# A four-layer trunk on one core: the root's wait placed later, weight blocks split two ahead, high and low parts stored apart, scores of two heads in turn

## The reference

```python
for i in range(4):
    x = x + 0.5 * swiglu(rms_norm(x, g1[i]), w_gate1[i], w_up1[i], w_down1[i])   # D_FF = 2816
    h = rms_norm(x, g_mix[i])
    x = x + (fox, conv, diff, fox)[i](h)
    x = x + 0.5 * swiglu(rms_norm(x, g2[i]), w_gate2[i], w_up2[i], w_down2[i])

def swiglu(h, wg, wu, wd):
    return (silu(h @ wg) * (h @ wu)) @ wd

# fox, for each of 16 heads of 64 features, causal:
s = q @ k.T / 8 + cum[q] - cum[k];  o = softmax(s) @ v
# diff, for each of 8 heads with two score maps each:
a = softmax(s1) - lam * softmax(s2);  o = a @ v
```

## Time and profile before

| What | Value |
|---|---|
| time, median of 3 runs | 2146.58 us |
| time of the profiled execution | 2145.89 us |
| span in the profile | 2144.1 us |
| TensorE busy | 2059.0 us (96%) |
| VectorE busy | 1478.0 us (69%) |
| ScalarE busy | 1062.4 us (50%) |
| GpSimd busy | 118.6 us (6%) |
| DMA traffic | 344.28 MB, mean 161 GB/s |
| mean granted clock of TensorE | 0.982 |

### The profile page before, as it was taken

The page is one execution under the profiler, slowest core; times in us unless marked ns, Lnnn a source line. Parts: engine busy times, 40 slices in busy tenths (PEclk is TensorE's granted clock), DMA queues, the critical chain, the costliest instruction groups (busy, mean ns, idle before and its releaser), DMA issues.

```text
span 2144.1 us, 28806 instructions
## 1 busy us (share of the span) xinstructions
PE 2059.0 (96%) x12322; PEld 1792.1 (84%) x12322; DVE 1478.0 (69%) x1750; ACT 1062.4 (50%) x1243; POOL 118.6 (6%) x118
## 2 busy tenths in 40 slices
PE   6999999999999997799999999989999999999999
PEld 5888888888788896788878888878887888888887
DVE  6766766776677499577657747877756765767773
ACT  5554555554554430555445535665535554455552
POOL 1000201000100112100000000010000000101000
PEclk8999999999999998999999999999999999999999
DMA  6555434555555540355556563346555555334553
GB/s 200 183 185 168 138 119 138 161 189 182 174 182 185 189 155 0 104 171 184 175 172 196 172 201 122 114 138 189 180 186 172 180 179 185 126 99 144 190 181 114
DMA packets 329692, 344.28 MB, mean 161 GB/s; under 512 B 8277, under 2 KB 325214, under 8 KB 329566
## 3 DMA queue, kind: packets, MB, share of 16 engines
q1 hardware_dynamic: 329422, 342.41, 50.3%
q10 hardware_dynamic: 144, 0.05, 0.0%
HBM read 341.38 MB, written 1.05 MB: 160 GB/s over the span
## 4 chain that ended last, share of the span: by engine, by line
PE 90%; DVE 6%; ACT 2%; issue 2%; DMA 0%; DVEq 0%; SPq 0%
PE banks L1326 47%; PE banks L1321 23%; PE banks L1310 5%; PE banks L1312 4%; PE banks L1311 4%; DVE sb_w_low L727 2%; PE banks L1504 2%; DVE sb_x_square L1201 2%; PE banks L1552 1%; ACT sb_w_high L436 1%; PE banks L1519 1%; PE banks L1536 1%; PE banks L1507 1%; DMA sb_raw<-in_ffn_w_up 0%; PE banks L1650 0%
## 5 line engine op out<-in xcount | busy, mean ns | idle before, releaser
L1326 PE MATMUL banks<-sb_x_both,sb_w_high 128*128 128x512 f32 x2816 | 979.8, 401 | 45.9 <-DVE sb_w_low L727 38.8
L727 DVE TENSOR_TENSOR sb_w_low<-sb_raw,sb_w_high 128x2048 fp32r<-128x2048 f32 (+1 forms) x332 | 747.1, 2252 | 154.9 <-ACT sb_w_high L436 153.3
L1321 PE MATMUL banks<-sb_x_both,sb_w_low 128*128 128x256 f32 x2816 | 735.6, 282 | 0.0
L436 ACT ACTIVATE sb_w_high<-sb_raw 128x2048 fp32r<-128x2048 f32 (+1 forms) x332 | 617.1, 1863 | 125.8 <-DMA sb_raw<-in_ffn_w_down 106.6
L1326 PEld LDWEIGHTS banks<-sb_x_both,sb_w_high 128*128 128x128 f32 x2816 | 512.6, 191 | 146.7 <-issue 49.2
L1321 PEld LDWEIGHTS banks<-sb_x_both,sb_w_low 128*128 128x128 f32 x2816 | 540.1, 192 | 31.7
L1326 PE MATMUL banks<-sb_h_both,sb_w_high 128*128 128x512 f32 x1408 | 495.3, 398 | 1.9 <-DVE sb_w_low L727 1.9
L1321 PE MATMUL banks<-sb_h_both,sb_w_low 128*128 128x256 f32 x1408 | 386.1, 282 | 0.0
L1326 PEld LDWEIGHTS banks<-sb_h_both,sb_w_high 128*128 128x128 f32 x1408 | 261.7, 189 | 61.1 <-DVE sb_w_low L727 2.2
L1321 PEld LDWEIGHTS banks<-sb_h_both,sb_w_low 128*128 128x128 f32 x1408 | 265.1, 188 | 6.0
L1310 PE MATMUL banks<-sb_x_both,sb_w_high 128*128 128x256 f32 x512 | 149.5, 292 | 0.0
(11 more groups left out here) (205 smaller groups left out, 2083.4 us busy)
## 6 DMA issues: line engine op xcount, KB each, us to landing
sb_raw<-in_ffn_w_gate SPq DMA_DIRECT2D x88, 1024.0 KB, 5.3
sb_raw<-in_ffn_w_up SPq DMA_DIRECT2D x88, 1024.0 KB, 5.3
sb_raw<-in_ffn_w_down SPq DMA_DIRECT2D x64, 1024.0 KB, 5.2
sb_raw<-in_ffn_w_down SPq DMA_DIRECT2D x32, 768.0 KB, 4.8
sb_raw<-in_fox_w_in SPq DMA_DIRECT2D x24, 1024.0 KB, 5.3
sb_raw<-in_conv_w_pw SPq DMA_DIRECT2D x12, 1024.0 KB, 5.6
sb_raw<-in_diff_w_in SPq DMA_DIRECT2D x12, 1024.0 KB, 5.1
sb_raw<-in_fox_w_out SPq DMA_DIRECT2D x8, 1024.0 KB, 4.9
```

The costliest lines, as they stand in the source:

```text
L436: act.activation(slot(w_high, b)[:, 0:width(b)], slot(raw, b)[:, 0:width(b)], ACT.Copy).then_inc(S["high_ready"], 1)
L727: dve.tensor_tensor(slot(w_low, b)[:, 0:width(b)], slot(raw, b)[:, 0:width(b)], slot(w_high, b)[:, 0:width(b)].bitcast(F32), ALU.subtract) ...
L1321: pe.matmul(bank[at][:, SEQ:2 * SEQ], low[:, n * P:(n + 1) * P], m_both[:, 0, :], start=False, stop=False, skip_group_check=True)
L1326: ins = pe.matmul(pair(bank[at][:, :]), high[:, n * P:(n + 1) * P], m_both[:, :, :], start=first, stop=last, skip_group_check=True)
```

## The change

**The root's wait.** TensorE no longer waits for `root_ready` after the first pair, but before the last of the four tiles of the second pair (its up tile into bank 3).

**Two blocks ahead.** ScalarE splits b+2 and b+3 before the root, VectorE before the reciprocal. In the pair loop the splits are now b+2p+4 and b+2p+5, each behind the evacuation of one half (ScalarE) or its first use (VectorE). The down projection has one split less in its first tile. In phase 0 the turning of the vectors moves from tile 0 to tile 1, and VectorE's tables from ahead of the down projection's splits to behind those of tile 1.

**Parts stored apart.** `x_both` and `h_both` had the high and the low part of a tile side by side; now all high parts come first and then all low parts. The 512-column matmul reads two runs of 256 columns that lie 8 KB (x) or 22 KB (h) apart.

**Scores of two heads in turn.** `score_pair` replaces two calls of `head_scores`: 128 columns of the one head, 128 of the other, 256 of the one, 256 of the other, and then the bf16 matmuls of both. In fox the second pair moves from around the sum for q into the value projection, nine matmuls after its start; in diff the second pair stands where head 2 stood.

```diff
-        x_both = sb("x_both", [P, KT, 2, SEQ], F32R)
+        x_both = sb("x_both", [P, 2, KT, SEQ], F32R)
...
-            h_both = during_ffn.enter_context(nc.sbuf_tensor("sb_h_both", [P, FF_TILES, 2, SEQ], F32R))
+            h_both = during_ffn.enter_context(nc.sbuf_tensor("sb_h_both", [P, 2, FF_TILES, SEQ], F32R))
...
+                if phases[i] == "ffn":
+                    split_high(starts[i] + 2)
+                    split_high(starts[i] + 3)
...
                 act.wait_ge(S["sumsq_done"], i + 1)
...
-                split_high(b + 2)
                 for p in range(PAIRS):
-                    split_high(b + 2 * p + 3)
                     upper_half(p, 0)
+                    split_high(b + 2 * p + 4)
                     silu(p)
-                    split_high(b + 2 * p + 4)
                     upper_half(p, 1)
+                    split_high(b + 2 * p + 5)
                     high(p)
...
-                split_low(b + 2)
                 for p in range(PAIRS):
                     gate(p)
-                    split_low(b + 2 * p + 3)
+                    split_low(b + 2 * p + 4)
                     scaled(p)
                     up(p)
-                    split_low(b + 2 * p + 4)
+                    split_low(b + 2 * p + 5)
                     low(p)
...
                 for T in range(3):
-                    for k in range(3):
+                    for k in range(0 if T else 1, 3):
                         split_low(e + 3 * T + 3 + k)
+                    if i == 0 and T == 1:
+                        before_tables()
...
                         for n in range(2):
+                            if p == 1 and which and n:
+                                pe.wait_ge(S["root_ready"], i + 1)
                             ins = tile(which, p, n, range(KT))
...
                 sum_squares(i, 3)
-                pe.wait_ge(S["root_ready"], i + 1)
...
+                    else:
+                        pe.wait_ge(S["masked"], c)
                         if fox:
+                            pe.wait_ge(S["probsT_ready"], turned_before[i] + 4 * g + 2 + 4 * u)
+                    parts = ((0, slice(0, P), P), (1, slice(P, 384), SEQ))
+                    for qb, cols, keys in parts:
+                        for m in range(2):
+                            rows = slice(HEAD * m, HEAD * m + HEAD)
+                            q = qT[rows, r * SEQ + qb * P:r * SEQ + (qb + 1) * P]
+                            ins = pe.matmul(bank[4 + m][:, cols], q, kT[rows, r * SEQ:r * SEQ + keys],
+                                            start=qb == 0, stop=not fox, skip_group_check=True)
...
-                    tokens_half(bank[2], v_blk, 0)
+                    tokens_half(bank[2], v_blk, 0, range(3))
+                    if j:
+                        score_pair(1, g, u)
+                    tokens_half(bank[2], v_blk, 0, range(3, KT))
```

More of the change, by code:

```diff
@@ L490, in high @@
                     act.wait_ge(S["hidden_ready"], PAIRS * f + p + 1)
-                    act.activation(h_both[:, 2 * p:2 * p + 2, 0, :], pair(hidden[:, :]), ACT.Copy
+                    act.activation(h_both[:, 0, 2 * p:2 * p + 2, :], pair(hidden[:, :]), ACT.Copy
                                    ).then_inc(S["h_high_ready"], 1)
-                split_high(b + 2)
                 for p in range(PAIRS):
-                    split_high(b + 2 * p + 3)
                     upper_half(p, 0)
+                    split_high(b + 2 * p + 4)
                     silu(p)
-                    split_high(b + 2 * p + 4)
                     upper_half(p, 1)
+                    split_high(b + 2 * p + 5)
                     high(p)
@@ L795, in boundary @@
                 x_lows(i, 3)
+                if phases[i] == "ffn":
+                    split_low(starts[i] + 2)
+                    split_low(starts[i] + 3)
                 width = SEQ + 2 if phases[i] in ("fox", "diff") else SEQ
@@ L889, in low @@
                     dve.wait_ge(S["h_high_ready"], PAIRS * f + p + 1)
-                    dve.tensor_tensor(h_both[:, 2 * p:2 * p + 2, 1, :], pair(hidden[:, :]),
-                                      h_both[:, 2 * p:2 * p + 2, 0, :].bitcast(F32),
+                    dve.tensor_tensor(h_both[:, 1, 2 * p:2 * p + 2, :], pair(hidden[:, :]),
+                                      h_both[:, 0, 2 * p:2 * p + 2, :].bitcast(F32),
                                       ALU.subtract).then_inc(S["h_low_ready"], 1)
-                split_low(b + 2)
                 for p in range(PAIRS):
                     gate(p)
-                    split_low(b + 2 * p + 3)
+                    split_low(b + 2 * p + 4)
                     scaled(p)
                     up(p)
-                    split_low(b + 2 * p + 4)
+                    split_low(b + 2 * p + 5)
                     low(p)
                 e = b + 2 * PAIRS
-                if i == 0:
-                    before_tables()
-                elif i == 2:
+                if i == 2:
                     after_tables()
                 for T in range(3):
-                    for k in range(3):
+                    for k in range(0 if T else 1, 3):
                         split_low(e + 3 * T + 3 + k)
+                    if i == 0 and T == 1:
+                        before_tables()
                     update_x(i + 1, T)
@@ L1476, in ffn @@
                         down(T, c)
-                        if i == 0 and T == 0 and c == 1:
+                        if i == 0 and T == 1 and c == 0:
                             pe.wait_ge(S["hidden_ready"], PAIRS)
@@ L1486, in attention, with score_pair @@
                 per = 4 if fox else 2
-                def head_scores(m, g, u):
-                    c = 16 * a + 4 * g + m + 4 * u
-                    dst = bank[4 + m % 2]
-                    if m == 0:
+                def score_pair(r, g, u):
+                    c = 16 * a + 4 * g + 2 * r + 4 * u
+                    if r == 0:
                         pe.wait_ge(S["q_ready"], 4 * a + g + u + 1)
@@ L1496, in head_scores @@
                             pe.wait_ge(S["neg_cum_ready"], GROUPS * w + g + u + 1)
-                    if fox and m == 3:
-                        pe.wait_ge(S["probsT_ready"], turned_before[i] + 4 * g + 2 + 4 * u)
-                    if m >= 2:
-                        pe.wait_ge(S["masked"], c - 1)
-                    tile, r = m // 2, slice(HEAD * (m % 2), HEAD * (m % 2) + HEAD)
-                    for qb, cols, keys in ((0, slice(0, P), P), (1, slice(P, 384), SEQ)):
-                        q = qT[r, tile * SEQ + qb * P:tile * SEQ + (qb + 1) * P]
-                        ins = pe.matmul(dst[:, cols], q, kT[r, tile * SEQ:tile * SEQ + keys], start=True, stop=not fox)
-                        if fox:
-                            at = u * (4 * SEQ) + (4 * g + m) * SEQ
-                            ins = pe.matmul(dst[:, cols], ones_bf[:, :], neg_cum_wide[:, bass.ds(at, keys)],
-                                            start=False, stop=True)
@@ L1509, in head_scores @@
-                    ins.then_inc(S["scores_done"], 1)
+                    else:
+                        pe.wait_ge(S["masked"], c)
+                        if fox:
+                            pe.wait_ge(S["probsT_ready"], turned_before[i] + 4 * g + 2 + 4 * u)
[6 more added lines that the diff above has]
+                                            start=qb == 0, stop=not fox, skip_group_check=True)
+                            if qb and not fox:
+                                ins.then_inc(S["scores_done"], 1)
@@ new lines, in score_pair @@
+                    if fox:
+                        for m in range(2):
+                            at = u * (4 * SEQ) + (4 * g + 2 * r + m) * SEQ
+                            for qb, cols, keys in parts:
+                                ins = pe.matmul(bank[4 + m][:, cols], ones_bf[:, :],
+                                                neg_cum_wide[:, bass.ds(at, keys)], start=False, stop=True,
+                                                skip_group_check=True)
+                            ins.then_inc(S["scores_done"], 1)
@@ L1680, in attention @@
                     turn(1, g, 0)
-                    head_scores(2, g, 0)
-                    head_scores(3, g, 0)
+                    score_pair(1, g, 0)
                     o_block(1)
@@ L1695, in attention @@
                         diff_group(j)
[L1696 to L1697 removed]
+                    score_pair(0, g, 0)
                     o_sums(g - 1, 0)
```

23 lines of the change are left out of this document (7 added, 16 removed).

## The result

The changed kernel takes 2072.42 us (median of four runs, 2072.31 to 2072.52), the kernel before 2146.0 us (2143.12 to 2146.94) beside it: a ratio of 0.9659, 95% interval 0.9643 to 0.9676. The forecast was 2071.6 us. The span is 2070.6 us, 73.5 us less, and the mean granted clock is 0.992 instead of 0.982.

A forecast was written before the change was run, and what follows sets the result against it. TensorE bounds the kernel, pausing 40.7 us for VectorE's low parts. Gains of 38.8 + 17.1 + 1.9 + 14.5 + 2.0 = 74.3 us from 2145.9 us gave 2071.6 us, range 2048 to 2097 us.

The forecast's parts named there:

- Terms 1 and 2: Starts of the eight ffn phases: TensorE's pauses go, 38.8 us, and the low clock behind them, 17.1 us.
- Term 3: First ffn phase's down projection: moving vectors and tables one tile later removes a pause, 1.9 us (ends 0 and 3.5).
- Term 4: Fox phases: scores of two heads run side by side, less new waits, gaining 14.5 us (ends 8 and 23).
- Term 5: Diff phase: scores of heads 2 and 3 paired in three groups, gaining 2.0 us (ends 0 and 2.5).
- Term 6: Wide matmuls reading parts stored apart: no effect taken; bounds 127 us won and 42 us lost.
- A: Rival: the layout pays some 5 ns in each wide couple, 21 us, giving 2050 us; chance 0.13.
- B: Rival: the layout costs 0.01 us in each wide couple, 42 us, giving 2114 us; chance 0.06.
- D: Rival: the ffn pause only moves, low part of b+2 still late, 28 us left, giving 2100 us; chance 0.06.
- C: Rival: new waits drop the fox inner groups to the low clock, costing 9.4 us, giving 2081 us; chance 0.09.
- E: Rival: ffn pair loop becomes the bound at ScalarE's split ahead of `silu`, 80 us, giving 2152 us; chance 0.04.

The follow-up runs named there:

- e7: Kernel before with only the vectors' turning and the tables of the first ffn phase one tile later: 2140.33 us, ratio 0.9991.
- e9: Kernel before with only block b+2 split ahead of the root, pair loop unchanged, and the root's wait moved to the second pair: 2098.21 us.
- e2: Kernel before with only the root's wait moved to the second pair's last tile, splits still behind the root: 2145.38 us, ratio 1.0004.
- e4: Kernel before with only the scores of two heads in turn, in fox and diff: 2128.93 us, ratio 0.993.
- e6: Kernel before with only the high and low parts of x and h stored apart: 2142.63 us, ratio 1.0001.
- e1: Kernel before with only the later root wait, two blocks split ahead of the root and the pair loop one block further: 2082.9 us, ratio 0.9715.
- e11: Changed kernel with six more VectorE operations of 128 x 512 in each pair: 2229.21 us, ratio 1.0394.
- e5: Changed kernel with the high and low parts of x and h side by side again: 2071.47 us, ratio 0.9661.
- e10: Changed kernel with two more VectorE operations of 128 x 512 in each pair: 2072.45 us, ratio 0.9661.
- e3: Changed kernel with the root's wait back behind the first pair, splits still ahead of the root: 2077.55 us, ratio 0.9687.

## Why the prediction was right

**Terms 1 and 2 (pauses 38.8, low clock 17.1; together 55.9).** The ffn phases are 61.4 us shorter. The first one's tables are 3.6 of them (e7), which leaves 57.8. The step held as worked out: low parts done 1.2 us before the sum, all 38.8 us gone, clock 1.00. A term that the working left out is the 0.26 us that a pause costs besides itself (e9), eight times. The clock's part is then 57.8 - 38.8 - 2.1 = 16.9 us, for 17.1. So close a match is in part luck, for it is one execution against one: the ffn phases of e2, e4 and e6, whose pauses are before's, are together 0.3 to 2.9 us shorter than before's, by stretches of low clock that differ from execution to execution.

**Term 3 (tables, 1.9).** The pause went and took its stretch of low clock with it: 3.6 us, at the upper end of 3.5. That size holds for this execution of before. The same pause is in e4, with no low clock behind it (window behind the pause, before and then e4, in the columns of the earlier trace rows):

```profile
169.34:177.34 8.00, 8.00 (x37) 6.93 (x38) 6.00 (x6) 2.82 (x4) 0.74 (x1) 0.79 0.34 116
...
169.50:177.50 8.00, 7.97 (x45) 6.98 (x46) 6.02 (x6) 2.80 (x4) 0.74 (x1) 1.00 0.43 137
```

The reason given was one of two: e7 shows that the move suffices, e1 that it is not needed.

**Term 4 (fox scores, 14.5).** This is the term that was mis-sized: 11.25 us. Between phases of the same kind the change gives 6.1 us (e4 and e11: 138.7 us against 144.8), where 7.25 were worked out. The pair itself was right (1.12 us for 1.2), the head's delay exact (4.55 us for 4.55), and the two waits nearly (0.80 and 0.26 us for 0.7 and 0.6). What failed is the sum over the groups, "3 x 1.5 + 2.9": in e4 against before, the three inner groups keep 0.92, 1.57 and 1.33 us and the last one 2.30 us. The first has a wait of 0.4 us for turns and the last one of 0.73 us for a copy of probabilities, neither of which the working had. The rest of the shortfall is the longer `sb_qT`, which the changed kernel met twice and which costs it 1.7 us a phase (the 0.9 us ahead of the scores, 0.94 instead of 0.4 us at the turns, and getting going again). In the first phase, before had the shorter one, so 6.1 - 1.7 = 4.4 us are left. In the second, before had the longer one too, where it cost 0.95 us (e1 against before: 145.78 and 144.83 us), with 3.4 us of low clock behind it, and the gain is 6.8 us.

**Term 5 (diff, 2.0).** 1.95 us. The eight passes of two heads side by side, read from the earlier trace rows, are the right price, and diff's own pairs gained nothing from the turn-taking.

**Term 6 (layout, 0, bounds -127 and +42).** Nothing, by e5 and e6. These bounds made the range wide, and the trace could not narrow them.

**The sum.** Terms 1 and 2 gave 1.9 us more than worked out, term 3 1.7 us more, term 4 3.25 us less, and the conv phase and the start took 1 us back. So the mechanism was right, but that the total came within 1 us of the forecast is luck: errors of up to 3 us cancelled.

**The rivals.** A and B fall by e5 and e6, D by the waits. C falls too: the stretch with the 0.80-us wait in it, and the rest of both fox phases, is at 1.00 (window in the columns of the earlier trace rows).

```profile
278.00:281.00 3.00, 2.20 (x17) 1.44 (x13) 1.92 (x7) 2.97 (x9) 0.00 (x0) 1.00 0.03 5
```

That the Trainium skill (TensorE: Matmul & The Clock Gate, Part 4) does not count transposes as busy in the same way would have spoken for C; here the sums, the values and the projection stood around the waits as well, so no run shows the rule at work or fails it. E has its mechanism (e11) but not its place: the loop has 2.56 us a pair to spare. My two reasons against it were that VectorE's waits overlap with those that it has anyway, and that TensorE holds two blocks in stock. The first is what e10 shows, as far as two operations. The second is no cover at all once the slack is used up (e11), since the banks stop TensorE first.

The conv phase is 0.9 us longer, with 23.9 us at 1.2 GHz in it instead of 20.5. It has 17.1 us in e1 and 20.5 us in e4, where its own code is the same, so I put this down to variation from one execution to the next, which is argued and not shown.

## What to carry to other kernels

When the engine that bounds a kernel waits for a chain, look at what each link's engine did just before. Here both were idle ahead of the root (ScalarE 6.86 us, VectorE 7.50 us), and the order of their instructions alone made the pause. Moving a wait does nothing while another input is later (e2), and the same move pays once that input is early (e3). How far ahead a block has to be is a number to test at one and at two, since each covers other stretches (e9), and the slack that a loop has is the waits of the engine in question, against the nearest buffer that it frees (e10, e11).

## What the runs showed of the hardware

- A pause costs more than itself: 0.26 us besides after 0.99 us (e9), and after 4.85 us some 2 us by the low clock (3 to 6 us of work at 0.50 behind each). After pauses of 0.6 us (e3) and 0.99 us at the phase starts (e9) the granted clock stayed at 1.00, but after one of 0.9 us in the second fox phase of e9 it was 0.79 over 8 us, and not after the same pause in its first. After the tables' 1.92 us it was 0.79 in before and 1.00 in e4. So the length of the pause alone does not decide it.
- Two fp32 matmuls over 64 rows each run side by side when they lie on different halves of the rows, whether the heads are given one after the other (diff before, eight passes in 0.86 us) or in turn (fox after). At 1395.62 us in diff before, the second head's first pass starts 0.01 us behind the first head's first and 0.20 us ahead of the first head's second, which the program gives earlier. The Trainium skill (TensorE: Matmul & The Clock Gate, "What overlaps and what doesn't") has matmuls in strict program order; these rows differ, and they decide.
- A matmul of 512 columns that reads two runs 8 or 22 KB apart starts at the same distance as one that reads them side by side (350 and 353 ns a couple).
- A VectorE operation of 128 x 512 took 0.75 or 2.49 us beside a GpSimd operation that started 0.05 us later in both cases. With that tie alone a fox phase differs by 0.95 us in the order of before and by 1.7 us in the changed one, which is as much as a small change is worth, and it fell differently in kernels that have the same code there.
